# A two-block network: three sevens instead of two in each pair of w_down column chunks

## The reference, cut to what matters

```python
u = jax.nn.relu(rms_norm(h, mlp_norm_g) @ w_up)   # h 256 x 2048, w_up 2048 x 8192
h = h + (u * u) @ w_down                          # w_down 8192 x 2048
```

## Time and profile before

| | us |
|---|---|
| runs, median of 3 (lowest to highest) | 2504.21 (2503.29 to 2504.7) |
| profiled execution, span (the page gives no other time of it) | 2504.0 |
| PE busy | 2480.6 |
| DVE busy | 1753.6 |
| ACT busy | 1257.8 |

### The profile page before, as it was taken

How to read it: one execution, slowest core, us unless ns; L and a number is a source line. 1 busy time by engine, 2 the same in 40 slices (tenths; PEclk the granted TensorE clock), 3 DMA queues, 4 the chain that set the end, 5 groups by cost and what they waited for, 6 DMA issues and landing times.

```text
span 2504.0 us, 38061 instructions
## 1 busy us (share of the span) xinstructions
PE 2480.6 (99%) x15416; PEld 2115.6 (84%) x15416; DVE 1753.6 (70%) x1978; ACT 1257.8 (50%) x1506; POOL 29.5 (1%) x26
## 2 busy tenths in 40 slices
PE   9999999999999999999999999999999999999998
PEld 7888888888888888888888888888888888888886
DVE  6656765668668677675777777775776666777777
ACT  7655344544444444445555555544654444444543
POOL 0000000000000000000000000000000000000000
PEclk9999999999999999999999999999999999999999
DMA  9454545546546546555545454556465565556553
GB/s 381 153 183 152 176 153 193 176 164 223 193 161 231 187 171 211 193 195 183 185 153 185 153 185 153 185 170 195 150 217 185 186 200 187 183 194 198 186 188 127
DMA packets 128239, 465.97 MB, mean 186 GB/s; under 512 B 14368, under 2 KB 14624, under 8 KB 127168
## 3 DMA queue, kind: packets, MB, share of 16 engines
q1 hardware_dynamic: 127920, 463.53, 55.2%
q10 hardware_dynamic: 144, 0.02, 0.0%
HBM read 461.39 MB, written 2.10 MB: 185 GB/s over the span
## 4 chain that ended last, share of the span: by engine, by line
PE 94%; issue 4%; DVE 2%; ACT 0%; DMA 0%; SPq 0%; DVEq 0%; POOL 0%; POOLq 0%
PE job L970 30%; PE job L982 16%; PE job L938 11%; PE job L940 11%; PE job L939 11%; PE job L957 2%; PE job L958 2%; PE job L959 2%; PE att L958 2%; PE att L957 2%; PE att L959 2%; PE att L1177 1%; PE att L998 0%; DVE w_low L1593 0%; PE att L1010 0%
## 5 line engine op out<-in xcount | busy, mean ns | idle before, releaser
L1274 ACT ACTIVATE w_high<-raw 128x1024 fp32r<-128x1024 f32 (+1 forms) x883 | 919.6, 1050 | 733.9 <-PE job L940 292.4
L1593 DVE TENSOR_TENSOR w_low<-raw,w_high 128x1024 fp32r<-128x1024 f32 (+1 forms) x883 | 1047.0, 1212 | 310.5 <-ACT w_high L1274 231.0
L970 PE MATMUL job<-actA,w_high 128*128 128x512 f32 x3328 | 798.3, 391 | 0.1
L970 PEld LDWEIGHTS job<-actA,w_high 128*128 128x128 f32 x3328 | 611.8, 188 | 119.9 <-issue 0.7
L982 PEld LDWEIGHTS job<-actA,w_low 128*128 128x128 f32 x3328 | 426.7, 191 | 16.2
L982 PE MATMUL job<-actA,w_low 128*128 128x256 f32 x3328 | 431.7, 283 | 0.0
L1796 DVE TENSOR_TENSOR slots<-job,slots 128x512 f32<-128x512 f32 x102 | 70.5, 691 | 344.1 <-ACT slots L1466 343.5
L938 PE MATMUL job<-w_high,actB 128*128 128x512 f32 x736 | 288.6, 392 | 2.5 <-DVE w_low L1593 2.0
L939 PE MATMUL job<-w_low,actB 128*128 128x512 f32 x736 | 287.1, 390 | 0.0
L940 PE MATMUL job<-w_high,actB 128*128 128x512 f32 x736 | 287.0, 390 | 0.0
L938 PE MATMUL job<-w_high,actA 128*128 128x512 f32 x576 | 230.9, 401 | 0.0
(11 more groups left out here) (257 smaller groups left out, 1906.0 us busy)
## 6 DMA issues: line engine op xcount, KB each, us to landing
raw<-in_weights SPq DMA_DIRECT2D x855, 512.0 KB, 4.2
M<-in_mem_t SPq DMA_DIRECT2D x8, 256.0 KB, 8.0
slots<-in_mem SPq DMA_DIRECT2D x2, 1024.0 KB, 12.2
M<-in_x_t SPq DMA_DIRECT2D x4, 512.0 KB, 13.8
H<-in_x SPq DMA_DIRECT2D x2, 1024.0 KB, 9.0
out<-H SPq DMA_DIRECT2D x8, 256.0 KB, 3.2
slots<-in_w_small SPq DMA_DIRECT2D x1, 1024.0 KB, 9.7
slots<-in_post_mix_g SPq DMA_DIRECT2D x1, 1024.0 KB, 4.3
```

Source lines behind the costliest of these rows:

```text
L970: mm = nc.tensor.matmul(J[job.buf][:, x, :], w_high[:, w % AHEAD, cols], act_both[job.act][:, c, :, :].rearrange("p a t -> p (a t)"), star ...
L1274: nc.scalar.activation(w_high[:, s % AHEAD, cols], raw[:, s % RAW_SLOTS, cols], ACT.Copy)\
L1593: nc.vector.tensor_tensor(w_low[:, s % AHEAD, cols], raw[:, s % RAW_SLOTS, cols], w_high[:, s % AHEAD, cols].bitcast(F32), ALU.subtract).t ...
```

## The change

- The order of pairs: before, sevens are pairs 0 and 1, after one and after three eights; now pairs 0, 1 and 2, after two and after three eights, and the third directly behind the second. A job has 22 windows (was 20) and 61 products (was 62).
- Pair 2 belongs to the second 512 hidden units, so `u_forms` runs twice a block: for pairs 0 and 1 after the first up job, for pair 2 after the second.
- The banks of C are laid out by token tile, so that two column chunks of one tile are neighbours, and `add_quads` does two adds of 1,024 columns where it did four of 512; in `add_sevens` two adds of the same operand become one with a broadcast operand.
- A kind of pair named "dma" is provided for (its `w_low` would be made by a DMA that adds), with its waits (`low_made`, `LOWS`, `by_dma`); no pair of the order is of that kind. Waits on `low_ready` keep their values; `sums_of` has a second one.

```diff
-QUAD_ORDER = (("eight", 2), ("seven", 0), ("eight", 3), ("eight", 4), ("seven", 1), ("eight", 5), ("eight", 6), ("eight", 7))
+QUAD_ORDER = (("eight", 3), ("eight", 4), ("seven", 0), ("eight", 5), ("seven", 1), ("seven", 2), ("eight", 6), ("eight", 7))
 SEVENS = [p for what, p in QUAD_ORDER if what == "seven"]
+FORM_JOBS = sorted({p // 2 for p in SEVENS})
...
-            if j == 0:
-                p.put(job.end + 2, "u_forms", b)
+            if j in FORM_JOBS:
+                p.put(job.end + 2, "u_forms", j)
...
+        def forms_of(ap, j):
+
+            mine = [SEVENS.index(p) for p in SEVENS if p // 2 == j]
+            return ap.rearrange("p (f q t) -> p f q t", f=4, t=P)[:, :, mine[0]:mine[-1] + 1, :]
...
+        def low_made(engine, w):
+
+            if by_dma(w):
+                engine.wait_ge(rest_landed[w % AHEAD], 16 * SLOT_DMA_LOWS[w])
+            else:
+                engine.wait_ge(low_ready, LOWS[w])
...
             if what == "C":
-                return J[buf][:, x[0], :] if i == 0 else att[:, 2 * buf + x[0], :]
+                return J[buf][:, i, :] if x[0] == 0 else att[:, 2 * buf + i, :]
...
-                        once("forms_low", job.needs[1] + 1)
+                        once("forms_low", len(FORM_JOBS) * job.needs[1] + FORM_JOBS.index(where // 2) + 1)
...
-                    nc.scalar.activation(forms_high, forms, ACT.Copy).then_inc(S["forms_high"], 1)
+                    nc.scalar.activation(forms_of(forms_high, a[0]), forms_of(forms, a[0]), ACT.Copy).then_inc(S["forms_high"], 1)
...
-                dve.wait_ge(low_ready, s + 3 - RAW_SLOTS)
+                low_made(dve, s + 1 - RAW_SLOTS)
+                low_made(dve, s + 2 - RAW_SLOTS)
...
-                    s1, s2, s3, s4 = (forms[:, i * T:(i + 1) * T].rearrange("p (q t) -> p q t", q=2) for i in range(4))
+                    s1, s2, s3, s4 = (to[:, i] for i in range(4))
...
-                    nc.vector.tensor_tensor(forms_low, forms, forms_high.bitcast(F32), ALU.subtract)\
+                    nc.vector.tensor_tensor(forms_of(forms_low, j), to, forms_of(forms_high, j).bitcast(F32), ALU.subtract)\
                         .then_inc(S["forms_low"], 1)
...
-                    nc.vector.scalar_tensor_tensor(hh(1, 0), u_two, r1, hh(1, 0), ALU.mult, ALU.add)
-                    done(nc.vector.scalar_tensor_tensor(hh(1, 1), u_two, r1, hh(1, 1), ALU.mult, ALU.add))
+                    both = hh(1, 0, 2).rearrange("p (i n) -> p i n", i=2)
+                    done(nc.vector.scalar_tensor_tensor(both, u_two.unsqueeze(1).to_broadcast([P, 2, COLS]), r1, both,
+                                                        ALU.mult, ALU.add))
...
-                    for i in range(2):
-                        for t in range(TT):
-                            hh = H[:, t, (c + i) * COLS:(c + i + 1) * COLS]
-                            ins = nc.vector.scalar_tensor_tensor(hh, quad_bank(buf, ("C", i, t)), rstd2[:, t:t + 1], hh,
-                                                                 ALU.mult, ALU.add)
+                    for t, banks in enumerate((J[buf][:, :, :], att[:, 2 * buf:2 * buf + 2, :])):
+                        hh = H[:, t, c * COLS:(c + 2) * COLS].rearrange("p (i n) -> p i n", i=2)
+                        ins = nc.vector.scalar_tensor_tensor(hh, banks, rstd2[:, t:t + 1], hh, ALU.mult, ALU.add)
```

More of the change, by code:

```diff
@@ L120, in products @@
         what, p, i = self.parts[k]
-        if what == "eight":
+        if what != "seven":
             return [(("C", i, x), ("u", 2 * p + cc, x), cc) for cc in range(2) for x in range(TT)]
@@ L508, in part_of, with by_dma @@
     return job.parts[k][2] if job.kind == "quads" and job.parts[k][0] == "seven" else None
+def by_dma(w):
+    job, k = WINDOW[w]
+    return job.kind == "quads" and job.parts[k][0] == "dma"
+LOWS = list(itertools.accumulate(int(not by_dma(w)) for w in range(PLAN.windows)))
+DMA_LOWS = list(itertools.accumulate(int(by_dma(w)) for w in range(PLAN.windows)))
+SLOT_DMA_LOWS = [sum(map(by_dma, range(w % AHEAD, w + 1, AHEAD))) for w in range(PLAN.windows)]
 SUMS = list(itertools.accumulate(int(part_of(w) == 1) for w in range(PLAN.windows)))
@@ L620, in build @@
         act_high, act_low = ({n: act_both[n][:, :, part, :] for n in "AB"} for part in (0, 1))
-        forms_both = sb("forms_both", [P, 2, 1024], F32R)
+        forms_both = sb("forms_both", [P, 2, 4 * len(SEVENS) * P], F32R)
         H = sb("H", [P, TT, D])
@@ L690, in build @@
         post_g = a2(6)
-        forms, forms_high, forms_low = m_slot(0), forms_both[:, 0, :], forms_both[:, 1, :]
-        form_at = lambda f, p: slice(((f - 1) * 2 + SEVENS.index(p)) * P, ((f - 1) * 2 + SEVENS.index(p) + 1) * P)
+        forms, forms_high, forms_low = Mf[:, 0:4 * len(SEVENS) * P], forms_both[:, 0, :], forms_both[:, 1, :]
+        form_at = lambda f, p: slice(((f - 1) * len(SEVENS) + SEVENS.index(p)) * P,
+                                     ((f - 1) * len(SEVENS) + SEVENS.index(p) + 1) * P)
+        def forms_of(ap, j):
+            mine = [SEVENS.index(p) for p in SEVENS if p // 2 == j]
+            return ap.rearrange("p (f q t) -> p f q t", f=4, t=P)[:, :, mine[0]:mine[-1] + 1, :]
         p1, u_one, u_two = slots[:, 4, 0:COLS], slots[:, 4, COLS:2 * COLS], slots[:, 5, 0:COLS]
@@ L722, in build @@
         sums_made = sem("sums_made")
+        negated, rest_landed = sem("negated"), [sem(f"rest_landed{i}") for i in range(AHEAD)]
         out_ready, half_done, wide_done = sem("out_ready"), sem("half_done"), sem("wide_done")
@@ L773, in load @@
                 if w >= RAW_SLOTS:
-                    sp.wait_ge(low_ready, w - RAW_SLOTS + 1 + (part_of(w - RAW_SLOTS) == 0))
+                    low_made(sp, w - RAW_SLOTS + (part_of(w - RAW_SLOTS) == 0))
                 sp.dma_start(raw[:, w % RAW_SLOTS, :], d["weights"][LOAD_AT[w] - 1]).then_inc(raw_loaded[w % RAW_SLOTS], 16)
@@ L853, in stage, with split @@
                                             ALU.pow).then_inc(S["rstd"], 1)
-            walk(n, lambda w: None, lambda w, s: None, stage)
+            def split(w, s):
+                if by_dma(s):
+                    pool.wait_ge(negated, DMA_LOWS[s])
+                    nc.gpsimd.dma_start(w_low[:, s % AHEAD, :].bitcast(F32), raw[:, s % RAW_SLOTS, :],
+                                        accum_op=ALU.add).then_inc(rest_landed[s % AHEAD], 16)
+            walk(n, lambda w: None, split, stage)
         @block.tensor
@@ L928, in products @@
                 if w > 0:
-                    pe.wait_ge(low_ready, w + 1)
+                    pe.wait_ge(low_ready, LOWS[w])
                 for cc, c in enumerate(chunks_of(w)):
@@ L946, in quads @@
                 first_of(w)
-                pe.wait_ge(low_ready, w + 1)
+                if by_dma(w):
+                    pe.wait_ge(high_ready, w + 1)
+                low_made(pe, w)
                 for x, (bank, (of, i, where), cc) in enumerate(job.products(k)):
@@ L1268, in split @@
                 if s >= AHEAD and WINDOW[s - AHEAD][0].kind == "features":
-                    act.wait_ge(low_ready, s - AHEAD + 1)
+                    act.wait_ge(low_ready, LOWS[s - AHEAD])
                     act.wait_ge(wide_done, WIDE[s - AHEAD])
@@ L1275, in split @@
                     .then_inc(high_ready, 1)
+                if by_dma(s):
+                    nc.scalar.activation(w_low[:, s % AHEAD, :], raw[:, s % RAW_SLOTS, :], ACT.Copy, scale=-1.0)\
+                        .then_inc(negated, 1)
             as_att = lambda: att[:, 2:4, :]
@@ L1586, in split @@
                     return
+                if by_dma(s):
+                    return
                 if part_of(s) == 1:
@@ L1889, in stage @@
                     wait(dve, n, "forms_high", 0)
-                    u = a_slot(2).rearrange("p (q c x t) -> p q c x t", q=2, c=2, x=TT)
+                    j, to = a[0], forms_of(forms, a[0])
+                    u = a_slot(2 + j % 2).rearrange("p (q c x t) -> p q c x t", q=2, c=2, x=TT)
+                    u = u[:, [p % 2 for p in SEVENS if p // 2 == j][0]:[p % 2 for p in SEVENS if p // 2 == j][-1] + 1]
                     a11, a12, a21, a22 = (u[:, :, c, x, :] for x, c in ((0, 0), (0, 1), (1, 0), (1, 1)))
-                    s1, s2, s3, s4 = (forms[:, i * T:(i + 1) * T].rearrange("p (q t) -> p q t", q=2) for i in range(4))
+                    s1, s2, s3, s4 = (to[:, i] for i in range(4))
                     done(nc.vector.tensor_tensor(s1, a21, a22, ALU.add))
```

## The result

The changed kernel takes 2515.7 us (median of 4 runs, 2514.2 to 2517.7) against 2504.5 beside it: a ratio of 1.0045 [1.0031, 1.0060], +11.3 us where +4.2 was forecast, and outside the range. The profiled execution has a span of 2514.7 us against 2504.0. The profiled run itself took 2516.6 us, about 2 more than its span; the prediction added 0.2 to its span, which shifts its absolute time but not the difference.

The account below looks back on a forecast made before the run. The prediction took PE, busy 99%, to bound the kernel, held only by late w_low. Its terms, -4.8 - 6.6 + 8.3 + 7.3 = +4.2 us, gave 2508.4 us, range 2503.5 to 2513.5.

Parts of the forecast that it names:

- Products removed: In the seven quad jobs: one block product fewer per job, 3 matmuls, 7 x 0.68 = -4.8 us.
- Two eights first: First seven of the four jobs behind an up job: both old PE stalls go, 4 x 1.66 = -6.6 us.
- A seven right behind a seven: Third seven's second window, jobs behind an up job: late w_low stalls PE 2.1 us each, 4 x 2.1 = +8.3 us.
- 1,024-wide sums, banks, waits: Wide adds in add_quads and add_sevens, new bank mapping, extra low_ready wait: nothing further counted, 0, with small bounds.
- Forms: Second u_forms per block, in the up stretch: hidden behind busy PE, 0, at most 1 us.
- The three second jobs: Quad jobs following another quad job: DVE enters late, so w15 stalls 2.4 us each, 3 x 2.4 = +7.3 us.
- rival C: Second job's start: if w_low(22) starts after 42.3, PE waits there too and more at w15; 2512 us, chance 0.18.
- the prediction's own sign of being wrong: Quad jobs: early w_low(15), a stall at w18 or w22, or PE waits in the up stretch would refute the forecast.
- Sum: Whole kernel: -4.8 - 6.6 + 8.3 + 7.3 = +4.2 us, span 2508.2, median 2508.4 us.
- Rival B: Quad jobs: DVE keeps up with two sevens in a row, PE's saving is all; 2492.8 us, chance 0.09, full or half.

Follow-up runs that it names:

- e7: The changed kernel with only two sevens, two eights ahead of them, and each seven's sums made before its first window's w_low: 2498.0 us.
- e5: The changed kernel, its three sevens kept, with each seven's sums made before its first window's w_low and that raw slot freed earlier: 2492.7 us.
- e2: The changed kernel with two sevens only (pairs 0 and 1) and two eights ahead of them, wide adds kept: 2497.7 us.
- e4: The changed kernel with the third seven's four sums made for one column only, leaving out part of that pair's weight sums: 2496.5 us.
- e3: The changed kernel with the old order of pairs, keeping the wide adds, new banks and extra waits: 2504.2 us.
- e1: The changed kernel, but the raw slot of a seven's first window may be reloaded once the four sums reading it are made: 2509.4 us.
- e8: The e5 kernel with w_low of the third seven's second window made three times over in all seven jobs: 2512.7 us.
- e9: The e5 kernel with w_low of the third seven's second window made four times over in all seven jobs: 2530.0 us.
- e6: The changed kernel with an eight between the second and third seven: 2520.7 us.

## Why the prediction was wrong

In the quads stretch of the trace the account is -4.76 (products) - 6.69 (old waits) + 24.41 = +13.0, where the prediction had -4.8 - 6.6 + 15.6 = +4.2. Point by point:

- *Products removed*, -4.8: right (e7 and e5 job by job, 7 x 0.68; their medians differ by 5.3).
- *Two eights first*, -6.6: right, and shown alone by e2 (-6.5).
- *A seven right behind a seven*, 2.1 us in each of four jobs: right. Measured 1.93 + 0.13; w_low(10) at 15.00, w_low(15) at 27.88 for 27.9. e4 and e5 show from two sides that DVE's list does it.
- *1,024-wide sums, banks, waits*, 0: right (e3). *Forms*, 0: right (89.04 us with one set and with two). An add of 1024 is 1.28 us, add_quads 2.38 from 596.76 to 599.14 for 2.3 to 2.4.
- *The three second jobs*, 2.4 us each: mis-sized. The waits at w15 were 2.88, 2.59 and 2.74, each with 0.13 behind it, 1.3 us more in all, since w_low(10) came at 16.03, 15.63 and 15.77 for 15.3. Each link ahead of it was a little late: w_low(5) stood at 10.56, 9.89 and 9.91 for 9.7, so the load for w10 went out at 11.8, 11.1 and 11.2 for 10.9, and it took 3.1 to 3.5 us. In the first job the load for w20 took 5.4 us to land for 3.2 to 3.3, and ACT waits 3.29 us for it (timeline of ACT):
```profile
583.36 1.06 ACT L1309 ACTIVATE w_high<-raw 128x1024 fp32r<-128x1024 f32 x1 [3.29 <-DMA raw<-in_weights]
```
  w_low(22) was then at 43.36, past the 42.3 that rival C named as its point, and PE waited there too, 1.25 us (1.13 and 0.12 behind it). In the third and fifth job the same load took 3.2, and the next job started at 43.59 for 43.6. C's wait at a job's start so came in one place of three, and with it the prediction's own sign of being wrong, a stall at w22. With the slot freed earlier (e1) both parts go. Why that load was slow stays open, but it is no accident of one execution: in e4, e8 and e9 the first job's load that goes out when w_low(15) is made took 5.1, 5.4 and 5.3 us.
- **The step that failed**: the step "Sum" put every PE wait at its own length and 0.13 us, and the clock after it at nothing, without a reason. At each of the three longest waits the clock fell to 0.50 for 3.4 or 6.8 us, behind two of them and before the end of the third, and matmuls stood 0.427 us apart for 0.227: 1.62, 1.59 and 2.90 us, 6.1 in all. That is 70% of the 8.8 us that were missing (the rest: 1.3 at w15, 1.25 at w22, and hundredths). The 6.1 are those of the profiled execution. In others of the same kernel more or fewer waits may be followed by it; the four runs lie 3.5 us apart. The trace of before held the sign of it, and I read from the clock only its mean. PE has two waits there with a bracket of 1.9 us or more, the one at 11.8 us shown above and this one, and each has a stretch of 3.4 us at 0.50 (from 13.2 and from 1757.4):
```profile
1757.56 3.50 PE L998 MATMUL att<-ident,H 128*128 128x128 f32 x16 [3.78 <-DVE H L1985]
```

Rival B was wrong for this kernel but its number, 2492.8, was right for the kernel in which DVE does not idle behind the sums (e5, 2492.7). The prediction said that neither order nor slots let DVE do any of its list earlier; for the order as coded that held, but the sums need no slot of PE's, and making them first takes the idle 1.13 us away.

## What to carry to other kernels

When an engine that is ahead by a bounded number of buffers falls behind in one kind of step, write its list of starts against the consumer's for the worst run of such steps: here it gave the place and the length of a wait to 0.1 us in the four jobs whose list had no late load in it, and 0.3 to 0.6 us too little in the three that had. Then look in that list for work that waits for nobody and put it where the engine idles; one such move turned +11 us into -12. And price a wait of 2 us and more of a busy TensorE above its length: here the longer ones cost 1.6 to 2.9 us on top, though not each time.

## What was not expected of the hardware

- Equal waits of PE do not have equal cost. Of the eighteen waits of 1.92 to 2.02 us in the quads jobs (four in the changed kernel, seven each in e1 and e8) four were followed by 3.4 us at half clock. Of the seventeen of 2.6 to 3.6 us in or right behind these jobs (three in the changed kernel, seven each in e6 and e9) ten had 3.4 or 6.8 us of it. What decides between equal ones is open.
- Up to the last 15 us of the program every half-clock stretch in the eleven traces begins during a PE wait with a bracket of 1.76 us or more, or less than 1.6 us behind it. No wait with a bracket of 0.9 to 1.65 us has one, that at w22 (1.13 us, bracket 0.97) included. The 3.78 us wait of the second block (L998 in before) has one in all eleven. In e2, e3, e5 and e7, without long waits in the quads jobs, there is none in these jobs.
- A wait costs 0.13 to 0.15 us beyond its own length at full clock (read over the six matmuls behind it).
- A 512 KB load that is issued while no other is under way lands in 3.1 to 3.6 us as a rule, but between 540 and 1140 us of the changed kernel four of 56 took 4.2 to 5.4 us, and in before one of 47 took 4.6.
